# The first modulation projection in two column halves, with the first projection steps between them

## The chip, the cores and the metric

The kernel runs on one core of a Trainium2 chip. The metric is device time in microseconds for one execution. Engines are named as the profile names them: PE (TensorE matmul) and PEld (its weight load), DVE (VectorE), ACT (ScalarE), POOL (GpSimd), SP (the sync engine, which here issues most DMAs).

## What is computed

One encoder layer on two groups of 1024 tokens with 1024 features each. What matters here is its start: a modulation vector from the condition `c`, and the modulated, normalised input that the input projection multiplies.

```python
mod = (jax.nn.silu(c) @ w_ada + b_ada).reshape(B, N_MOD, D_MODEL)[:, :, None, :]
shift1, scale1, gate1, shift2, scale2, gate2 = [mod[:, i] for i in range(N_MOD)]
h = rmsnorm(x, g_pre_mix) * (1 + scale1) + shift1
x = x + gate1 * rmsnorm(token_mixer(h, w_in, ...), g_post_mix)   # token_mixer starts with h @ w_in
h = rmsnorm(x, g_pre_ffn) * (1 + scale2) + shift2
x = x + gate2 * rmsnorm(expert_choice_moe(h, ...), g_post_ffn)
```

`w_ada` is 1024 by 6144 in float32. The first 2048 of its columns give shift1 (0 to 1023) and scale1 (1024 to 2047) and are needed before any `h` exists. The other 4096 are needed later.

## The kernel before

All five engines run hand-written programs in one block, each in its own order, and they meet in counted semaphores. There is no scheduler: the order in the code is the order on each engine. Work is cut along the 1024 features into KC = 8 steps k of 128, and along tokens into quarters q of 512 (q 0 and 1 are the first group).

**SP** issues, in order and from one queue: `c_in`, the first token quarter x(0) (2 MB), the eight pieces `a_w[:, k, :]` of the first modulation weights (L646, 1 MB each, k-th 128 rows, all 2048 columns), and w(0), the first half unit of the input projection weights (L488, 1 MB). Next comes x(1), in the same buffer as x(0): its issue (L482) waits until PE has turned all eight k of x(0) (`turned` 8). Then w(1), the gate weights, the gate biases.

**PE** first does `ada(0, k)` for k 0 to 7 (L1749): four matmuls with M = 2 rows each (the two groups), 512 columns wide, one in each 32-column group of the array, summed over k in bank PO. A pair of k shares one semaphore (`a_first`). Between them, for k 2 to 5, come the transposes of x(0), two k at a time (`turn_x`, L1738; four transposes for each k, into banks 0 and 1 in turn). After them come 8 filler transposes (`keep_awake`), the 16 small transposes that turn the modulation row into columns (L1923), 18 fillers, and then `stream`: for each k the six matmuls of blocks 0 and 1 (L1805), each k waiting for `h_ready`. Before block b of 2 and up, PE waits for `w_lo_ready` of its half unit and for `evac_done` b - 1, since the two banks are used in turn (L1815, L1816). Block 2 is the first to use w(1).

**ACT** squares x(0) in eight pieces (L1036), takes the turned x out of the banks (`take_x`, L1038), takes two of the four row pieces (`a_row_first`), rounds w(0) to `w_hi` (L1018, two pieces), and makes h in place (`make_h`, L1047). The squares of x(1) stand between the h of k 4 to 7 and behind them. Only after that comes its `fill` stream, whose first work is the evacuation of blocks 0 and 1 (L1030).

**DVE** normalises x(0), takes the other two row pieces, adds the bias and makes `scale` (L1571, L1575), then `w_lo` and, for each k, `h_hi` and `h_lo` (L1379, L1381). Then `mean_of(1)`, the `w_lo` of w(1), and the normalising of x(1). **POOL** makes the reciprocal roots (L792) and `w_hi` of w(1) (L803).

Of the kernel before, what the change touches and what calls it, by code (L numbers as in the profile page):

```python
# [8 lines left out]
ALU = mybir.AluOpType  # L9
# [213 lines left out]
def front(nc, io):  # L223

    with ExitStack() as ctx:
# [160 lines left out]
        a_row_ready, a_row_stored = sem("a_row_ready"), several("a_row_stored", 2)  # L386
# [24 lines left out]
        o_loaded, o_hi_ready, o_lo_ready = several("o_loaded", KC), sem("o_hi_ready"), sem("o_lo_ready")  # L411
# [6 lines left out]
        x1_half, h2_half = sem("x1_half"), sem("h2_half")  # L418
# [7 lines left out]
        PX = 7  # L426
        A_ROUNDS = 3
# [48 lines left out]
        def _(sp):  # L476
# [85 lines left out]
            def load_o(c):  # L562
                sp.wait_ge(blk_done, NBLK - 2 * (1 - c))
                for a in range(4):
                    sp.dma_start(o_raw[:, 2 * a:2 * a + 2, c * HALF:(c + 1) * HALF], w_out_view[a, c]).then_inc(o_loaded[4 * c + a], 16)
# [78 lines left out]
            load_x(0)  # L644
            for k in range(KC):
# [368 lines left out]
        def _(act):  # L1014
# [23 lines left out]
            def take_x(k):  # L1038
                act.wait_ge(turned, k + 1)
                nc.scalar.activation(h_raw[:, k, 0:HALF], ps[:, k % 2, :], ACT.Copy).then_inc(xT_ready, 1)  # L1040

            def a_row_first():
                act.wait_ge(a_done, KC)
                for j in range(2):
                    nc.scalar.activation(a_row[32 * j:32 * j + 2, 0, :], ps[32 * j:32 * j + 2, PO, :], ACT.Copy).then_inc(a_row_ready, 1)

            def make_h(q, k):  # L1047
                g, half = q // 2, q % 2
                cut = slice(half * HALF, (half + 1) * HALF)
# [83 lines left out]
            def stream():  # L1133
# [26 lines left out]
                for t in range(N_TILES + OUT_TAIL):  # L1160
# [25 lines left out]
                    if 1 <= t <= N_TILES:  # L1186
                        if t == N_TILES:
                            act.wait_ge(x1_half, 1)
# [25 lines left out]
            for k in range(KC):  # L1214
                take_x(k)
            act.drain()
            a_row_first()
            split_w(0, 0)
            for k in range(KC):
                make_h(0, k)  # L1220
                if k == 1:
                    split_w(0, 1)
                if k >= 4:
                    squares(1, k - 4)
# [133 lines left out]
        def _(dve):  # L1358
# [124 lines left out]
            def stream():  # L1483
# [23 lines left out]
                for t in range(N_TILES + OUT_TAIL):  # L1507
# [9 lines left out]
                    if 1 <= t <= N_TILES:  # L1517
# [4 lines left out]
                        for cut in HALVES_OF_D if t == N_TILES else (slice(0, D),):  # L1522
# [3 lines left out]
                            nc.vector.tensor_tensor(ox[:, j, cut], ox[:, j, cut], h2[:, j, cut], ALU.add).then_inc(x1_ready if cut.stop == D else x1_half, 1)  # L1526
# [22 lines left out]
                    if 1 <= t <= N_TILES:  # L1549
                        dve.wait_ge(or_ready, 2 * t)  # L1550
                        for cut in HALVES_OF_D if t == N_TILES else (slice(0, D),):
                            nc.vector.scalar_tensor_tensor(h2[:, j, cut], ox[:, j, cut], o_r[:, 1:2], rows[g][:, 1, cut], ALU.mult, ALU.mult)
                            dve.drain()
                            nc.vector.tensor_tensor(h2[:, j, cut], h2[:, j, cut], rows[g][:, 2, cut], ALU.add).then_inc(h2_ready if cut.stop == D else h2_half, 1)
# [11 lines left out]
            a_row_first()  # L1566
            dve.wait_ge(cols_loaded, 48)
            dve.wait_ge(mod_turned, 2)
            for g in range(GROUPS):
                turned_mods = ps[:, PS:PS + 4, 0:4 * GROUPS].rearrange("p j (k g) -> p j k g", g=GROUPS)[:, :, :, g]  # L1570
                nc.vector.tensor_tensor(mods[:, :, :, g].rearrange("p w (j k) -> p (w j) k", j=2), turned_mods,  # L1571
                                        b_cols[:, :].rearrange("p (j k) -> p j k", k=4), ALU.add)
            dve.drain()
            for g in range(GROUPS):
# [1203 lines left out]
```

## Time and profile before

| what | value |
|---|---|
| median of 3 runs | 2403.22 us (2403.15 to 2404.04) |
| the profiled execution, its own time | 2404.34 us |
| span in its trace | 2402.6 us |
| PE busy | 2296.1 us (96%) |
| DVE, ACT, POOL busy | 1208.7, 1103.8, 603.2 us |
| mean DMA rate | 213 GB/s |

Before its first matmul PE waits 14.5 us, the longest wait but one that it has. The stretch that the change touches is the first 51 us of the span, 2% of it: until PE begins block 2 at 51.05 us. Everything else (the other blocks, the recurrent and attention parts, the experts) comes later.

### The profile page before, as it was taken

What the parts mean: (1) busy time and instruction counts of PE and PEld (TensorE: products, weight loads), DVE (VectorE), ACT (ScalarE), POOL (GpSimd) and SP (SyncE); (2) the same over time, 40 slices, a digit from 0 to 9 for tenths busy, and PEclk for the clock granted to TensorE, in tenths of its full rate; (3) what the DMA queues carried; (4) which work ended last, traced back from release to release, by engine and by line L of the source; (5) the groups of instructions that cost most, each with busy time, mean ns of one, the idle gap of its engine ahead of it and who ended that gap; (6) DMA issues with size and microseconds to landing.
All of it is one profiled execution on the core that took longest, in us unless ns stands there. A gap on an engine that the chain in (4) does not pass through costs nothing. (4 is left out here: it accounts for less than half of the span.)

```text
span 2402.6 us, 35196 instructions
## 1 busy us (share of the span) xinstructions
PE 2296.1 (96%) x13583; PEld 1915.1 (80%) x13583; DVE 1208.7 (50%) x1881; ACT 1103.8 (46%) x1828; POOL 603.2 (25%) x676
## 2 busy tenths in 40 slices
PE   6999999999999999999947999999999999999997
PEld 4679989777899897667736888888888888888886
DVE  3222334554413346665566555544445556666655
ACT  4223444655433436665543444444444455555552
POOL 3004342443133324430021011111110122222434
PEclk9999999999999999999978999999999999999999
DMA  8835445658454459764547566666666678888785
GB/s 319 259 107 182 145 160 185 191 150 185 122 194 141 162 177 249 228 180 158 170 189 263 204 211 221 214 226 210 207 203 231 216 268 309 322 308 291 284 302 175
DMA packets 239040, 511.49 MB, mean 213 GB/s; under 512 B 36981, under 2 KB 128005, under 8 KB 235825
## 3 DMA queue, kind: packets, MB, share of 16 engines
q1 hardware_dynamic: 190960, 394.78, 49.0%
q0 software_dynamic: 47936, 114.77, 16.0%
q8 instruction: 93, 1.52, 0.3%
q14 instruction: 51, 0.41, 0.1%
HBM read 415.32 MB, written 93.69 MB: 212 GB/s over the span
## 5 line engine op out<-in xcount | busy, mean ns | idle before, releaser
L2492 DVE TENSOR_TENSOR moe_w_lo<-moe_wf,moe_w_hi 128x2048 fp32r<-128x2048 f32 x192 | 439.5, 2292 | 456.6 <-ACT moe_w_hi L2367 450.0
L2367 ACT ACTIVATE moe_w_hi<-moe_wf 128x2048 fp32r<-128x2048 f32 x192 | 367.8, 1916 | 551.4 <-PE moe_acc L2630 550.5
L2630 PE MATMUL moe_acc<-moe_w_hi,moe_x_hi 128*128 128x512 f32 x1024 | 401.7, 392 | 0.9 <-DVE moe_x_lo L2498 0.6
L2630 PE MATMUL moe_acc<-moe_w_hi,moe_x_lo 128*128 128x512 f32 x1024 | 398.9, 390 | 0.0
L2630 PE MATMUL moe_acc<-moe_w_lo,moe_x_hi 128*128 128x512 f32 x1024 | 398.4, 389 | 0.0
L2630 PEld LDWEIGHTS moe_acc<-moe_w_hi,moe_x_hi 128*128 128x128 f32 x1024 | 192.3, 188 | 40.7 <-DVE moe_x_lo L2498 0.8
L2630 PEld LDWEIGHTS moe_acc<-moe_w_hi,moe_x_lo 128*128 128x128 f32 x1024 | 192.2, 188 | 40.3
L2630 PEld LDWEIGHTS moe_acc<-moe_w_lo,moe_x_hi 128*128 128x128 f32 x1024 | 192.4, 188 | 38.9
L1793 PE MATMUL banks<-fr_w_hi,fr_h_hi 128*128 128x256 f32 x768 | 223.2, 291 | 0.0
L1793 PE MATMUL banks<-fr_w_lo,fr_h_hi 128*128 128x256 f32 x768 | 217.0, 283 | 0.0
L1793 PE MATMUL banks<-fr_w_hi,fr_h_lo 128*128 128x256 f32 x768 | 216.9, 282 | 0.0
L1784 PE MATMUL banks<-fr_h_hi,fr_w_hi 128*128 128x512 f32 x496 | 204.3, 412 | 1.9 <-DVE fr_h_lo L1381 1.1
L2630 PE MATMUL moe_acc<-moe_w_hi,moe_h_hi 128*128 128x512 f32 x512 | 199.3, 389 | 0.0
L2630 PE MATMUL moe_acc<-moe_w_hi,moe_h_lo 128*128 128x512 f32 x512 | 199.2, 389 | 0.0
L2630 PE MATMUL moe_acc<-moe_w_lo,moe_h_hi 128*128 128x512 f32 x512 | 199.2, 389 | 0.0
L1784 PE MATMUL banks<-fr_h_hi,fr_w_lo 128*128 128x512 f32 x496 | 194.2, 392 | 0.0
L1784 PE MATMUL banks<-fr_h_lo,fr_w_hi 128*128 128x512 f32 x496 | 193.7, 390 | 0.0
L1030 ACT ACTIVATE fr_stage<-banks 128x512 f32<-128x512 f32 (+1 forms) x114 | 67.3, 590 | 271.9 <-PE banks L1784 146.2
L1362 DVE TENSOR_TENSOR fr_w_lo<-fr_w_raw,fr_w_hi 128x1024 fp32r<-128x1024 f32 x56 | 73.6, 1316 | 208.3 <-ACT fr_w_hi L1018 208.3
L906 POOL DMA_DIRECT2D fr_v<-scratch_vov x224 | 156.5, 740 | 81.9 <-PE banks L1963 80.6
L1793 PEld LDWEIGHTS banks<-fr_w_hi,fr_h_hi 128*128 128x128 f32 x768 | 146.8, 191 | 4.9 <-issue 4.8
L1793 PEld LDWEIGHTS banks<-fr_w_lo,fr_h_hi 128*128 128x128 f32 x768 | 147.0, 191 | 0.1
(294 smaller groups left out, 4083.4 us busy)
## 6 DMA issues: line engine op xcount, KB each, us to landing
moe_wf<-in_w_expert_gate SPq DMA_DIRECT2D x64, 1024.0 KB, 4.9
moe_wf<-in_w_expert_up SPq DMA_DIRECT2D x64, 1024.0 KB, 4.9
moe_wf<-in_w_expert_down SPq DMA_DIRECT2D x64, 1024.0 KB, 5.8
fr_w_raw<-in_w_units SPq DMA_DIRECT2D x28, 1024.0 KB, 7.2
fr_bias<-in_na_bias SPq DMA_DIRECT2D x16, 1520.0 KB, 11.1
fr_a_w<-in_w_ada POOLq DMA_DIRECT2D x16, 1024.0 KB, 9.0
scratch_qk_t<-fr_stage SPq DMA_DIRECT2D x64, 256.0 KB, 2.5
scratch_vov<-fr_stage SPq DMA_DIRECT2D x96, 128.0 KB, 2.2
```

Source lines behind the costliest of these rows:

```text
L906: pool.dma_start(v[j][p0:CHUNK, CH_AT[rb] + n, :], v_view[2, m, r0:r0 + k, cols_, :]).then_inc(nv_loaded[j], 16)
L1030: nc.scalar.activation(out, product, ACT.Copy).then_inc(evac_done, 1)
L1362: nc.vector.tensor_tensor(w_lo[:, h % 2, k, :], w_raw[:, h % 2, k, :], w_hi[:, h % 2, k, :].bitcast(F32), ALU.subtract).then_inc(w_lo_read ...
L1784: mm = nc.tensor.matmul(ps[:, b % 2, :], w[x1][:, slot, k, a * P:(a + 1) * P], h[x2][:, k, t * HALF:(t + 1) * HALF], start=start, stop=stop)
L1793: mm = nc.tensor.matmul(ps[:, b % 2, part * QW:(part + 1) * QW], h[x1][:, k, tile:tile + P], w[x2][:, slot, k, :], start=(k == 0 and i == ...
L2367: nc.scalar.activation(w_hi[:, q, :, :], wf[:, q, :, :], ACT.Copy).then_inc(w_hi_ready, 1)
L2492: nc.vector.tensor_tensor(w_lo[:, q, :, :], wf[:, q, :, :], w_hi[:, q, :, :].bitcast(F32), ALU.subtract).then_inc(w_lo_ready, 1)
L2630: mm = nc.tensor.matmul(acc[:, j, b, :], x[:, g, k, :], w[:, q, a, h * HALF:(h + 1) * HALF], start=(k == 0 and i == 0), stop=(k == KC - 1 ...
```

## The change

The first modulation weights come in two halves. A half is 512 columns of shift1 and the same 512 of scale1, so half 0 gives the modulation of k 0 to 3 and half 1 that of k 4 to 7. SP issues eight half pieces (0.5 MB, in runs of 2 KB instead of 8 KB), then w(0), then the other eight, then x(1) as before behind `turned` 8. Each half is multiplied in four groups of 256 columns (`ada_first`), into bank PO (half 0) and PA = 3 (half 1). The row pieces, the turning and the DVE arithmetic are done once for each half (`a_row_first(half)`, `turn_mods(half)`, `modulation(half)`).

On PE, all of half 0 comes first, then the turning of x(0) for k 0 to 5, then 10 fillers, and then four rounds of: one step of `stream` (k 0 to 3), in rounds 1 and 2 one `turn_x` (k 6, 7), and two k of half 1. On ACT the h of a half follows its `take_x` and one piece of `split_w`, and all squares of x(1) come behind the last h. On DVE `mean_of(1)` moves behind the `w_lo` of w(1). Some semaphores are shared (the half pieces with the later output weights, `row_half` for two uses at the end of the front part), with counts changed to match.

```diff
-            for k in range(KC):
-                sp.dma_start(a_w[:, k, :], ada_view[k, :, 0:4 * HALF]).then_inc(a_first[k // 2], 16)
+                sp.dma_start(ada_part(a_w[:, k, :], 0), ada_part(ada_view[k, :, 0:4 * HALF], 0)).then_inc(a_first[k // 2], 16)
             load_w(0)
+            for k in range(KC):
+                sp.dma_start(ada_part(a_w[:, k, :], 1), ada_part(ada_view[k, :, 0:4 * HALF], 1)).then_inc(a_o_loaded[k], 16)
             load_x(1)
...
+            def ada_first(k, half):
+                if half:
+                    pe.wait_ge(a_o_loaded[k], 16)
+                else:
+                    pe.wait_ge(a_first[k // 2], 32)
+                for j in range(4):
+                    c0 = (j // 2 * 2 + half) * HALF + j % 2 * QW
+                    mm = nc.tensor.matmul(ps[32 * j:32 * j + 2, (PO, PA)[half], 0:QW], c_silu[:, k, :], a_w[:, k, c0:c0 + QW],
+                                          start=(k == 0), stop=(k == KC - 1))
+                mm.then_inc((a_early, a_done)[half], 1)
...
+            for k in range(6):
+                turn_x(0, k)
+                if k == 1:
+                    turn_mods(0)
+            keep_awake(PC[0], 10)
+            for k in range(4):
+                fill.tick(1)
+                if k in (1, 2):
+                    turn_x(0, 5 + k)
+                ada_first(2 * k, 1)
+                ada_first(2 * k + 1, 1)
+            keep_awake(PC[0], 8)
+            turn_mods(1)
+            keep_awake(PA, 18)
```

**ACT, from the first h to the evacuation of block 0, before.** L1054 makes h, L1036 squares x(1), L1030 evacuates a block.

```order
L1054 ACTIVATE fr_h_raw<-fr_h_raw,fr_mods,fr_scale 128x512 [waits fr_scale_ready] x2
L1018 ACTIVATE fr_w_hi<-fr_w_raw 128x1024 [waits fr_w_loaded0]
L1054 ACTIVATE fr_h_raw<-fr_h_raw,fr_mods,fr_scale 128x512 [waits fr_scale_ready] x3
L1036 ACTIVATE banks,fr_ss<-fr_x 128x512 [waits fr_x_loaded]
L1036 ACTIVATE banks,fr_ss<-fr_x 128x512
L1054 ACTIVATE fr_h_raw<-fr_h_raw,fr_mods,fr_scale 128x512 [waits fr_scale_ready]
L1036 ACTIVATE banks,fr_ss<-fr_x 128x512 [waits fr_x_loaded]
L1036 ACTIVATE banks,fr_ss<-fr_x 128x512
```

The same place now (L1065 makes h, L1049 takes turned x, L1055 the row pieces, L1045 squares, L1039 evacuates).

```order
L1065 ACTIVATE fr_h_raw<-fr_h_raw,fr_mods,fr_scale 128x512 [waits fr_scale_ready] x4
L1049 ACTIVATE fr_h_raw<-banks 128x512 [waits fr_turned] x4
L1027 ACTIVATE fr_w_hi<-fr_w_raw 128x1024 [waits fr_w_loaded0]
L1055 ACTIVATE fr_a_row<-banks 2x256 [waits fr_a_done]
L1055 ACTIVATE fr_a_row<-banks 2x256
L1065 ACTIVATE fr_h_raw<-fr_h_raw,fr_mods,fr_scale 128x512 [waits fr_scale_ready] x4
L1045 ACTIVATE banks,fr_ss<-fr_x 128x512 [waits fr_x_loaded]
```

Behind that row stand the other seven squares and then `L1039`, the evacuation of block 0, in both kernels. The squares of x(1) moved from between the h of k 4 to 7 to behind them.

**PE, from the fillers on, now.** L1756 is a filler, L1841 a stream step's matmul (six for each k), L1786 the modulation, L1766 a transpose of x(0).

```order
L1756 MATMUL banks<-fr_ident 128x128 x10
L1841 MATMUL banks<-fr_h_hi,fr_w_hi 128x512 [waits fr_h_ready,fr_w_lo_ready]
...
L1786 MATMUL banks<-fr_a_w,fr_c_silu 2x256 [waits fr_a_o_loaded0]
L1786 MATMUL banks<-fr_a_w,fr_c_silu 2x256 x3
L1786 MATMUL banks<-fr_a_w,fr_c_silu 2x256 [waits fr_a_o_loaded1]
L1786 MATMUL banks<-fr_a_w,fr_c_silu 2x256 x3
L1841 MATMUL banks<-fr_h_hi,fr_w_hi 128x512 [waits fr_h_ready]
...
L1766 MATMUL banks<-fr_ident,fr_x 128x128 [waits fr_xT_ready]
```

Before, all transposes of x(0) stood ahead of the last two k of the modulation, and every stream step behind it:

```order
L1736 MATMUL banks<-fr_ident 128x128 x10
L1758 MATMUL banks<-fr_a_w,fr_c_silu 2x512 [waits fr_a_first3]
L1758 MATMUL banks<-fr_a_w,fr_c_silu 2x512 x3
L1758 MATMUL banks<-fr_a_w,fr_c_silu 2x512 [waits fr_a_first3]
L1758 MATMUL banks<-fr_a_w,fr_c_silu 2x512 x3
L1736 MATMUL banks<-fr_ident 128x128 x8
L1923 MATMUL banks<-fr_ident,fr_a_row 128x2 [waits fr_a_row_ready]
```

The last two transposes of x(0), on which SP's issue of x(1) waits, moved behind stream steps 1 and 2.

## Rows read from the trace of the kernel before

**Rows 1.** The page: PE's busy time, and the chain that ended last.
```profile
PE 2296.1 (96%) x13583; PEld 1915.1 (80%) x13583; DVE 1208.7 (50%) x1881; ACT 1103.8 (46%) x1828; POOL 603.2 (25%) x676
PE 42%; DVE 3%; DMA 2%; issue 1%; POOL 0%; ACT 0%; DVEq 0%; POOLq 0%; ACTq 0%; SPq 0%
```

**Rows 2.** Timeline, PE, 14 to 57 us (start, us, engine line, tiles, idle before).
```profile
14.50 3.59 PE L1758 MATMUL banks<-fr_a_w,fr_c_silu 128*2 128x512 f32 x16 [14.50 <-DMA fr_a_w<-in_w_ada]
...
19.38 1.89 PE L1758 MATMUL banks<-fr_a_w,fr_c_silu 128*2 128x512 f32 x8 [1.07 <-DMA fr_a_w<-in_w_ada]
21.19 1.97 PE L1746 MATMUL banks<-fr_ident,fr_x 128*128 128x128 f32 x8
...
28.23 1.09 PE L1746 MATMUL banks<-fr_ident,fr_x 128*128 128x128 f32 x8
...
30.47 1.90 PE L1758 MATMUL banks<-fr_a_w,fr_c_silu 128*2 128x512 f32 x16
...
37.49 0.47 PE L1805 MATMUL banks<-fr_h_hi,fr_w_hi 128*128 128x512 f32 x1 [1.02 <-DVE fr_h_lo L1381]
...
45.11 0.39 PE L1805 MATMUL banks<-fr_h_hi,fr_w_lo 128*128 128x512 f32 x1
...
49.87 0.39 PE L1805 MATMUL banks<-fr_h_hi,fr_w_lo 128*128 128x512 f32 x1
51.05 0.50 PE L1784 MATMUL banks<-fr_h_hi,fr_w_hi 128*128 128x512 f32 x1 [0.79 <-DVE fr_w_lo L1362]
...
56.63 0.60 PE L1746 MATMUL banks<-fr_ident,fr_x 128*128 128x128 f32 x4
```

**Rows 3.** Windows: us, PE, PEld, DVE, ACT, POOL busy, PEclk, DMA share, GB/s.
```profile
9.00:14.00 5.00, 0.00 (x0) 0.00 (x0) 0.00 (x0) 4.21 (x12) 0.00 (x0) 1.00 1.02 428
14.00:19.00 5.00, 3.81 (x17) 0.61 (x17) 1.99 (x5) 1.57 (x6) 2.74 (x4) 1.00 1.02 426
36.00:40.00 4.00, 2.98 (x16) 2.37 (x15) 3.78 (x8) 3.92 (x6) 0.00 (x0) 1.00 1.03 343
```

**Rows 4.** The two issues of x (L482): first and last start; time to landing.
```profile
L482 SPq DMA_DIRECT2D fr_x<-in_x x2: 389/406/423, 1.2 to 29.3; - x2
...
DMA to landing us min/median/max: 8.1/8.7/9.3
```

**Rows 5.** The same for the two issues of w (L488).
```profile
L488 SPq DMA_DIRECT2D fr_w_raw<-in_w_units x2: 562/1126/1689, 6.1 to 29.8; - x2
...
DMA to landing us min/median/max: 11.6/11.6/11.6
```

**Rows 6.** Timeline, PE: matmuls of 256 columns in four groups, from 73.86 us.
```profile
73.86 0.61 PE L1779 MATMUL banks<-fr_h_hi,fr_wg 128*16 128x256 f32 x8
74.29 0.61 PE L1779 MATMUL banks<-fr_h_lo,fr_wg 128*16 128x256 f32 x8
```

**Rows 7.** Timeline, ACT and DVE, 24 to 37 us.
```profile
24.93 1.08 ACT L1040 ACTIVATE fr_h_raw<-banks 128x512 f32<-128x512 f32 x2 [1.14 <-PE banks L1746]
...
32.43 1.20 ACT L1045 ACTIVATE fr_a_row<-banks 2x512 f32<-2x512 f32 x2 [2.43 <-PE banks L1758]
...
35.02 1.22 DVE L1362 TENSOR_TENSOR fr_w_lo<-fr_w_raw,fr_w_hi 128x1024 fp32r<-128x1024 f32 x1
35.15 1.52 ACT L1054 ACTIVATE fr_h_raw<-fr_h_raw,fr_mods,fr_scale 128x512 f32<-128x512 f32 x2 [0.43 <-DVE fr_scale L1575]
36.16 0.42 DVE L1379 CAST fr_h_hi<-fr_h_raw 128x512 fp32r<-128x512 f32 x1
36.57 1.04 ACT L1018 ACTIVATE fr_w_hi<-fr_w_raw 128x1024 fp32r<-128x1024 f32 x1
36.66 0.69 DVE L1381 TENSOR_TENSOR fr_h_lo<-fr_h_raw,fr_h_hi 128x512 fp32r<-128x512 f32 x1
```

**Rows 8.** Timeline, ACT: first and last piece of the squares of x(0).
```profile
9.39 0.60 ACT L1036 ACTIVATE banks<-fr_x 128x512 f32<-128x512 f32 x1 [6.67 <-DMA fr_x<-in_x]
...
15.54 0.19 ACT L1036 ACTIVATION_READ_ACCUMULATOR banks<-fr_x 128x1 f32 x1
```

**Rows 9.** Timeline, all engines: what stands before block 2 and behind it.
```profile
41.45 2.43 POOL L803 CAST fr_w_hi<-fr_w_raw 128x1024 fp32r<-128x1024 f32 x2 [16.33 <-DMA fr_w_raw<-in_w_units]
...
48.64 2.35 DVE L1362 TENSOR_TENSOR fr_w_lo<-fr_w_raw,fr_w_hi 128x1024 fp32r<-128x1024 f32 x2
48.82 1.93 POOL L792 TENSOR_TENSOR fr_rms<-fr_mean,fr_mhalf 128x4 f32<-128x4 f32 x1 [4.42 <-DVE fr_mean L1369]
49.68 1.21 ACT L1030 ACTIVATE fr_stage<-banks 128x512 f32<-128x512 f32 x2 [1.39 <-PE banks L1805]
...
50.92 2.73 DVE L1373 TENSOR_SCALAR fr_x<-fr_x,fr_rms 128x1024 f32<-128x1024 f32 x4
```

More of the change, by code:

```diff
@@ L1213, in _ @@
                 squares(0, j)
-            for k in range(KC):
[L1215 to L1224, printed above, removed]
+            a_row_first(0)
+            for half in range(2):
+                for k in range(4 * half, 4 * half + 4):
+                    take_x(k)
+                act.drain()
+                split_w(0, half)
+                if half:
+                    a_row_first(1)
+                for k in range(4 * half, 4 * half + 4):
+                    make_h(0, k)
+            for j in range(4):
+                squares(1, j)
             act.wait_ge(cols_loaded, 48)
@@ L1565, in _ @@
             nc.vector.tensor_copy(b_cols[:, :], ps[:, PS, 0:2 * KC])
-            a_row_first()
             dve.wait_ge(cols_loaded, 48)
[L1568 to L1574, printed above, removed]
-                a = nc.vector.scalar_tensor_tensor(scale[:, g, :], mods[:, 1, :, g], 1.0, g_pre[:, :], ALU.add, ALU.mult)
-            a.then_inc(scale_ready, 1)
-            split_w(0, 0)
-            for k in range(KC):
-                split_h(0, k)
-                if k == 1:
+            for half in range(2):
+                a_row_first(half)
+                modulation(half)
+                if half == 0:
+                    split_w(0, 0)
+                for k in range(4 * half, 4 * half + 4):
+                    split_h(0, k)
+                if half == 0:
                     split_w(0, 1)
-            mean_of(1)
             for piece in range(2):
                 split_w(1, piece)
+            mean_of(1)
             for j in range(4):
@@ L1760, in ada, with turn_mods @@
                 mm.then_inc(a_done, 1)
+            def ada_first(k, half):
+                if half:
+                    pe.wait_ge(a_o_loaded[k], 16)
+                else:
+                    pe.wait_ge(a_first[k // 2], 32)
+                for j in range(4):
+                    c0 = (j // 2 * 2 + half) * HALF + j % 2 * QW
+                    mm = nc.tensor.matmul(ps[32 * j:32 * j + 2, (PO, PA)[half], 0:QW], c_silu[:, k, :], a_w[:, k, c0:c0 + QW],
+                                          start=(k == 0), stop=(k == KC - 1))
+                mm.then_inc((a_early, a_done)[half], 1)
+            def turn_mods(half):
+                pe.wait_ge(a_row_ready, 2 * half + 2)
+                for which in range(2):
+                    for k in range(4):
+                        at_ = slice(64 * which, 64 * which + 2)
+                        mm = nc.tensor.transpose(ps[:, MOD_BANKS[half][which], k * GROUPS:(k + 1) * GROUPS], a_row[at_, half, k * P:(k + 1) * P], ident[at_, at_])
+                mm.then_inc(mod_turned, 1)
             def turn_rows(g):
@@ L1867, in turn_h2 @@
                 if t == N_TILES - 1 and not half:
-                    pe.wait_ge(h2_half, 1)
+                    pe.wait_ge(row_half, 2)
                 else:
```

77 lines of the change are left out of this document (40 added, 37 removed).

## The prediction, made before the changed kernel was run

> **What bounds the kernel now.** I read the page first: PE is busy for 96% of the span, and the chain that ended last is almost all matmul where it names an engine [rows 1]. So the time is PE's work plus the few places where PE stands still, and a change at the start is worth exactly what it moves the moment from which PE runs on without a break. Next I read PE's timeline from the start [rows 2]. PE's first matmul comes at 14.50, the last two k of the modulation at 30.47, the first stream step at 37.49, the last matmul of the last step at 49.87, and block 2 begins at 51.05. From there on PE's order is the same in both kernels. So the question is one number: **when does block 2 begin**, against 51.05. The stretch is 51 of 2402.6 us, and 0.2% (4.8 us) is about what a measurement can tell from no change.
>
> The windows show what holds the start: the DMA engines are full, 426 to 428 GB/s from 9 to 19 us [rows 3]. The pairs of modulation weights (2 MB each) end 14.50 and 19.38, so 4.9 us for 2 MB.
>
> **The first stream step, now.** The bytes ahead of it shrink from x(0) plus 8 MB to x(0) plus 4 MB plus w(0).
> - x(0) is there at 9.39 [rows 8]. Four pairs of half pieces, 1 MB each, follow. At the rate of the 8 KB runs a pair takes 2.45 us (4.9 / 2). The new runs are of 2 KB, which no row shows alone. The other bound is the stretch from 36 to 40 us, in which w(1) comes in runs of 1 KB: 343 GB/s, 3.06 us for a pair [rows 3]. I take 2.6, nearer to the first, as x(0) with its 4 KB runs came at about that rate too. Last pair: 9.4 + 10.4 = 19.8 (19.2 to 21.6).
> - Two k of the modulation remain. Four groups of 256 columns take 0.43 us where PE is at speed (start to start) [rows 6]. At the start the same matmuls take double: 3.59 us for two k of 512 columns against 1.90 us later [rows 2]. PE will be idle about a third of the time until then, so I take the slow price, 0.9 each. End of half 0: about 21.5 (20.1 by the early bounds).
> - The transposes of x(0) come only now. Two k take 1.97 us in the slow state, 1.09 later [rows 2]: 23.4. ACT takes k 0 to 3 at 0.54 each [rows 7]; the third and fourth transpose wait for its first two, so the fourth is taken at about 25.5. Then ACT rounds the first piece of w(0), 1.05, which has landed (19.8 + 3.1 = 22.9, as one more MB at 343 GB/s): 26.6. DVE's `w_lo` 1.22, then `h_hi` and `h_lo`, 1.2 from the start of one to the end of the other [rows 7]: 29.0. If PE reaches its speed early, 27.6.
> - So the first stream step starts at S = 28.8, with ends 27.4 and 31.0 (the slow DMA bound). Before: 37.49. That part of the change is worth **8.7 us** if nothing came behind.
>
> **From there to block 2.** What lies behind S is PE's own row of work:
> - A stream step is six matmuls at 0.227 (45.11 to 49.87, 21 of them) [rows 2]: 1.36. Four steps 5.44. Eight k of half 1 at 0.43: 3.44, and two transposes of x(0) at 0.49: 0.98. End of half 1 at S + 9.9 = 38.7. The weights for it landed by about 34, so no wait for data. DVE delivers an h in 1.11, under 1.36.
> - Before, the end of the modulation (32.4) was followed by ACT's next h at 35.15, 2.8 us later [rows 7], with copies of 512 columns and 16 small transposes. With copies and transposes halved I take 2.1: S + 12.0. Four h at 0.75: S + 15.0. DVE adds 1.2 behind the first: PE's step for k 4 at S + 14.0, its last step ends at S + 19.5 = 48.3. Before it was 50.1. **On PE alone the gain has shrunk to 1.8 us**, or 2.8 with the 0.79 us wait at block 2, since PE now does the modulation and two transposes between the steps instead of ahead of them.
> - Block 2 also wants bank 0 evacuated, and that is **ACT's** work, behind all eight squares of x(1), which moved behind the last h. The eight squares take 6.34 us (9.39 to 15.73) [rows 8]. ACT starts them at S + 15.0, ends at S + 21.4, and the evacuation of one block, half of 1.21 [rows 9], ends at S + 22.0. Block 2 starts at **S + 22.1 = 50.9**. Before, ACT had idled 1.39 us ahead of that evacuation [rows 9], so it cost nothing there.
> - Could the squares start at all at S + 15.0? x(1) is issued when the eighth transpose is done, now behind stream step 2: S + 6.8 = 35.6, against 29.35 before. It lands 8.1 to 9.3 us later [rows 4]: S + 14.9 to S + 16.1. I take the first, since the queue has run empty by then, as it was for the first x. The other end costs 1.1 us more.
> - w(1) is issued behind it, at S + 7.2. Before it took 11.6 us behind a backlog [rows 5]. From x(1) on, 3 MB at 428 and 343 GB/s are 8 us and some 2 of start and end: S + 17.2. POOL rounds it, 2.43, DVE's second piece 1.2 behind [rows 9]: S + 21.0 = 49.8. Late too (before it had waited from 43.9 to 48.64 for DVE), but just behind ACT. `mean_of(1)` moving behind these two pieces costs nothing, as the squares end later still.
> - Behind block 2: mean, root (1.93 or less) and normalising (2.73) of x(1) [rows 9] end at S + 26.5 at the latest. PE wants x(1) 5.6 us after the start of block 2 [rows 2], S + 27.7. Covered, with 1.2 us to spare.
>
> The sum: block 2 at 50.9 against 51.05, **0.1 us earlier**. The span becomes 2402.5, the profiled time 2404.2. That execution lies 1.1 us above the median of the runs, so I forecast 2403.1 for the median. The shared semaphores, `row_half` among them, are waited for at the same places with counts that the same instructions reach: nothing. After block 2 all is the same order, shifted as one.
>
> The Trainium skill, page "DMA: Bandwidth & Descriptors", section "Bandwidth", speaks against cutting the loads: it wants 1 MiB or more in a DMA for 75% of peak, and gives 2.0 us plus bytes / 436e3 for one. By that a half piece is an estimated 3.2 us and a whole one 4.4. The rows don't bear it out for queued loads: 2 MB in 4.9 us is 2.45 for a whole piece.
>
> **The rivals.**
> 1. *The start comes early and part of the gain stays.* PE is at speed before the transposes and the half pieces keep the rate of the whole ones: S = 27.4, ACT's tail as above, block 2 at 49.5, 1.5 us earlier: 2401.7. If moreover x(1) were so quick that ACT never waits it stays at that, since ACT is bound by its own row; PE's own end (S + 19.5) can't be reached. For it: ACT's row is short of waits. Against: at the start PE is fed in pieces.
> 2. *Slower: the 2 KB runs come at the rate of the 1 KB ones.* The place is the last pair of half 0. At 3.06 us for a pair, and w(0) and x(1) landing at their late ends, S = 30.7, squares from S + 16.1, block 2 at 53.9: 2.9 us later, 2406.1. It decides against the change from about 2.65 us for a pair on (0.2 us above my 50.9 is all the room). For it: only rows at 1 KB and 4 KB or more exist.
> 3. *Each half piece pays a price of its own.* If every DMA cost a fixed 2 us that the queue doesn't hide, a half piece would take 3.2 us (2.0 and 1.2 of data) and half 0 would end at 35: S = 44, block 2 at 66, about 2418. Against it: the 2.45 us of a whole piece in the rows leaves no room for 2 us. This is what the page "DMA: Bandwidth & Descriptors" of the Trainium skill would give, section "Bandwidth".
> 4. *PE stays slow through the new gaps.* PE waits about 2 us between its fillers and S. If the stream steps and half 1 then run at the doubled price, S to S + 9.9 becomes S + 19.7, and all behind it 10 us later: 2413.
>
> **How the numbers follow.** My forecast, within about 1 us: 0.47. Rival 1: 0.22. Rival 2 (1 to 4.5 us slower): 0.22. Rivals 3 and 4: 0.02 and 0.05. Something larger in the gaining direction that I don't see: 0.02. The likeliest is 2403.1. The range takes in rivals 1 and 2 with the runs' own spread of 0.9 us: 2400.9 to 2406.2. That leaves out 3, 4 and the tails, under 0.2. Faster by over 0.2% (below 2398.4) needs more than the whole gain on PE: 0.03. Slower by over 0.2% (above 2408.0): rivals 3, 4 and the tail of 2, 0.09. Within: 0.88.
>
> **What would show it.** In the profile after: PE's first stream step at 27.4 to 31; half 1 done about 10 us later; the issue of x(1) near 35.6 and a hole in the DMA rate ahead of it; ACT's squares in one row from about 44 to 50; block 2 with a wait of 2 to 3 us that ends with ACT's evacuation, not with `w_lo`. If block 2 waits for nothing, my reading of ACT is wrong. If S is above 31, the runs of 2 KB are. If the two traces differ after block 2 by more than at it, the shift doesn't carry, and the whole argument from one number falls.

## The result, and the profile of the changed kernel

| | before | after |
|---|---|---|
| median of 20 runs | 2403.18 us (2401.22 to 2405.77) | 2407.59 us (2405.29 to 2412.69) |
| the profiled execution, its own time | 2404.34 us | 2407.66 us |
| span in its trace | 2402.6 us | 2405.9 us |
| block 2 begins | 51.05 us | 54.65 us |

The ratio is 1.002 with an interval of 1.0014 to 1.0027: slower by 4.4 us. The forecast was 2403.1 and its range ended at 2406.2, so it was wrong. Block 2 had been forecast at 50.9.

PE's timeline of the changed kernel answers to [rows 2]. Columns: start, us, engine line, tiles, idle before and what ended it.

```profile
14.84 1.89 PE L1786 MATMUL banks<-fr_a_w,fr_c_silu 128*2 128x256 f32 x16 [0.52 <-DMA fr_a_w<-in_w_ada]
17.55 1.89 PE L1786 MATMUL banks<-fr_a_w,fr_c_silu 128*2 128x256 f32 x16 [0.82 <-DMA fr_a_w<-in_w_ada]
20.27 1.89 PE L1786 MATMUL banks<-fr_a_w,fr_c_silu 128*2 128x256 f32 x16 [0.83 <-DMA fr_a_w<-in_w_ada]
...
24.52 2.46 PE L1766 MATMUL banks<-fr_ident,fr_x 128*128 128x128 f32 x12
...
30.77 0.47 PE L1841 MATMUL banks<-fr_h_hi,fr_w_hi 128*128 128x512 f32 x1 [1.85 <-DVE fr_h_lo L1393]
...
32.32 1.04 PE L1786 MATMUL banks<-fr_a_w,fr_c_silu 128*2 128x256 f32 x16
33.30 0.50 PE L1841 MATMUL banks<-fr_h_hi,fr_w_hi 128*128 128x512 f32 x1
...
41.85 1.09 PE L1756 MATMUL banks<-fr_ident 128*128 128x128 f32 x8
...
46.16 0.47 PE L1841 MATMUL banks<-fr_h_hi,fr_w_hi 128*128 128x512 f32 x1 [0.71 <-DVE fr_h_lo L1393]
...
54.65 0.50 PE L1820 MATMUL banks<-fr_h_hi,fr_w_hi 128*128 128x512 f32 x1 [2.79 <-DVE fr_w_lo L1374]
...
60.26 0.60 PE L1766 MATMUL banks<-fr_ident,fr_x 128*128 128x128 f32 x4
```

A reader should take five things from it. The pairs of half pieces come 2.7 us apart. The first stream step starts at 30.77 (S, as in the prediction), 6.7 us before the old 37.49. The four rounds behind it end at 41.85, at S + 11.1. The step for k 4 starts at 46.16, and the last step ends at 51.9. Then PE waits 2.79 us for `w_lo` of w(1), and block 2 begins 3.6 us later than before. From block 2 to the first transpose of x(1) it is 5.6 us, as in [rows 2].

The timeline of the other engines tells who was late. First SP's two issues, which came at 29.35 and 29.78 before:

```profile
38.42 0.37 SPq L488 DMA_DIRECT2D fr_x<-in_x  x1
38.83 0.55 SPq L494 DMA_DIRECT2D fr_w_raw<-in_w_units  x1
```

And what stands ahead of block 2 on POOL, DVE and ACT, the answer to [rows 9]:

```profile
50.36 2.02 POOL L812 CAST fr_w_hi<-fr_w_raw 128x1024 fp32r<-128x1024 f32 x2 [25.21 <-DMA fr_w_raw<-in_w_units]
...
51.43 3.16 DVE L1374 TENSOR_TENSOR fr_w_lo<-fr_w_raw,fr_w_hi 128x1024 fp32r<-128x1024 f32 x2 [2.11 <-POOL fr_w_hi L812]
```
```profile
46.99 0.60 ACT L1045 ACTIVATE banks<-fr_x 128x512 f32<-128x512 f32 x1
...
53.16 0.19 ACT L1045 ACTIVATION_READ_ACCUMULATOR banks<-fr_x 128x1 f32 x1
53.37 1.08 ACT L1039 ACTIVATE fr_stage<-banks 128x512 f32<-128x512 f32 x2
```

w(1) lands at 50.36, 11.5 us after its issue; its `w_lo` is ready at 54.59. ACT's row of squares runs from 46.99 to 53.35 without a gap, and the evacuation of block 0 is done at 53.9. So two chains end within 0.7 us of each other, and the one through w(1) is the later. The windows (columns as in [rows 3]) show the hole that the late issue leaves in the loads:

```profile
14.00:19.00 5.00, 3.65 (x37) 0.97 (x33) 1.93 (x5) 1.63 (x6) 2.68 (x4) 1.00 1.05 387
...
36.00:40.00 4.00, 4.00 (x37) 2.49 (x30) 0.00 (x0) 1.52 (x3) 0.00 (x0) 1.00 0.17 28
```

28 GB/s from 36 to 40 us, against 343 before [rows 3]; and 387 GB/s where the half pieces come (14 to 19 us), against 426 there before [rows 3].

### The profile page after: what moved, and what is told of

Its sections match the earlier page's. It is cut to its first block and busy times, and to the rows that moved or that the text cites. A ratio compares the mean times of both kernels' runs of the same rounds, so it can differ in the third digit from the quotient of the medians.

```text
span 2405.9 us, 35342 instructions
## 1 busy us (share of the span) xinstructions
PE 2301.4 (96%) x13647; PEld 1920.9 (80%) x13647; DVE 1205.0 (50%) x1887; ACT 1104.0 (46%) x1830; POOL 598.3 (25%) x676
## 5 line engine op out<-in xcount | busy, mean ns | idle before, releaser
L1039 ACT ACTIVATE fr_stage<-banks 128x512 f32<-128x512 f32 (+1 forms) x114 | 67.1, 590 | 271.4 <-PE banks L1820 147.0
```

Of the source, the lines that this page charges most:

```text
L1039: nc.scalar.activation(out, product, ACT.Copy).then_inc(evac_done, 1)
```

## The experiments

Beside each ran the kernel before, with medians of 2402.9, 2403.3 and 2402.7 us in the three sets of runs. "Block 2", "turn" and "span" are read from one profiled execution of each, in us; "turn" is the first transpose of x(1), which PE does when block 2 is through. The ratio is the 95% interval against the kernel before beside it.

| variant | from | block 2 | turn | span | median (lowest to highest) | ratio |
|---|---|---|---|---|---|---|
| before | | 51.05 | 56.63 | 2402.6 | 2403.18 | |
| after | | 54.65 | 60.26 | 2405.9 | 2407.59 | 1.0014 to 1.0027 |
| cut_loads | before | 52.96 | 58.54 | 2404.5 | 2404.97 (2402.94 to 2407.73) | 0.9995 to 1.0015 |
| squares_behind | before | 50.82 | 56.39 | 2401.9 | 2403.07 (2399.90 to 2406.35) | 0.9986 to 1.0005 |
| late_x1 | before | 53.13 | 61.05 | 2403.9 | 2406.34 (2404.05 to 2410.45) | 1.0005 to 1.0023 |
| w1_first | after | 54.38 | 61.44 | 2406.5 | 2407.93 (2405.02 to 2410.68) | 1.0006 to 1.0026 |
| turn_early | after | 52.89 | 58.46 | 2404.6 | 2404.59 (2403.49 to 2406.38) | 0.9996 to 1.0015 |
| warm_start | after | 55.45 | 62.58 | 2407.6 | 2409.38 (2406.69 to 2410.55) | 1.0011 to 1.0030 |
| fill_gap | after | 54.83 | 62.00 | 2407.9 | 2406.95 (2403.78 to 2410.69) | 1.0006 to 1.0024 |
| again | after | 54.60 | 61.76 | 2407.3 | 2408.53 (2404.14 to 2410.18) | 1.0011 to 1.0029 |
| hold_clock | after | 55.29 | 60.88 | 2403.9 | 2405.22 (2403.99 to 2406.49) | 1.0002 to 1.0020 |
| best1 | after | 51.44 | 58.59 | 2400.6 | 2403.34 (2400.67 to 2405.88) | 0.9989 to 1.0007 |
| best3 | after | 53.17 | 58.73 | 2403.9 | 2403.23 (2401.61 to 2406.17) | 0.9995 to 1.0013 |
| best5 | after | 50.26 | 56.60 | 2402.2 | 2402.33 (2400.97 to 2406.75) | 0.9993 to 1.0011 |

### What one part costs in the kernel before

**cut_loads** cuts only the loads: each 1 MB piece comes as two half pieces, and all of PE's work stays.

```diff
-                sp.dma_start(a_w[:, k, :], ada_view[k, :, 0:4 * HALF]).then_inc(a_first[k // 2], 16)
+                for half in range(2):
+                    sp.dma_start(ada_part(a_w[:, k, :], half), ada_part(ada_view[k, :, 0:4 * HALF], half)).then_inc(a_first[k // 2], 16)
```

> The kernel before with each of the eight 1 MB pieces issued as two half pieces in runs of 2 KB, both halves of a k one after the other, nothing else changed. Theory (the short runs are slower, 2.7 against 2.45 us for 1 MB): the last pair lands at 32.4 instead of 30.5, the first stream step at 39.4 and block 2 at 53.0. Rival (the runs cost nothing): 30.5, 37.5 and 51.05.

```profile
32.37 1.90 PE L1760 MATMUL banks<-fr_a_w,fr_c_silu 128*2 128x512 f32 x16 [0.73 <-DMA fr_a_w<-in_w_ada]
...
52.96 0.50 PE L1786 MATMUL banks<-fr_h_hi,fr_w_hi 128*128 128x512 f32 x1 [0.77 <-DVE fr_w_lo L1364]
```

The last pair is multiplied from 32.37 instead of 30.47 [rows 2], and block 2 follows 1.9 us later too. So 8 MB in runs of 2 KB cost 1.9 us more than in runs of 8 KB, 0.24 for each MB: half 0 of the changed kernel, 4 MB, pays an estimated 1.0 us. The cause (the runs' length or the number of DMAs, 16 for 8) was not told apart.

**squares_behind** moves only the squares and the mean of x(1), as the change does.

```diff
                 make_h(0, k)
...
-                if k >= 4:
-                    squares(1, k - 4)
+            for j in range(4):
+                squares(1, j)
...
-            mean_of(1)
             for piece in range(2):
                 split_w(1, piece)
+            mean_of(1)
```

> The kernel before with one part of the change alone: ACT's eight squares of x(1) behind the last h instead of between the h of k 4 to 7, and DVE's mean behind the rounding of w(1). Theory (ACT's row costs only because x(1) comes late in the changed kernel): x(1) is here by 38.7, the h are no longer held up, the last h is made by about 43, the squares end at 49.4, the rounding on DVE at about 49, block 2 at 50.2 instead of 51.05, 0.8 earlier. Rival (the move of the squares is itself the loss): block 2 at 52 or later.

```profile
50.82 0.47 PE L1784 MATMUL banks<-fr_h_hi,fr_w_hi 128*128 128x512 f32 x1 [0.17 <-ACT fr_stage L1030]
```

Block 2 begins at 50.82. With x(1) there in time, this move costs nothing. Where S is 37.9, ACT's row just fits. The theory had given it 0.8 us: the profile has 0.2 (0.6 counted from S, which came 0.4 us later here), the medians show no difference.

**late_x1** adds to it one wait on SP, which puts the issue of x(1) and w(1) about where the change put it.

```diff
             load_w(0)
+            sp.wait_ge(h_ready, 1)
             load_x(1)
```

> The kernel of squares_behind with SP's issue of x(1) and w(1) held until the first h is ready, about 37.5 instead of 29.35 us, as late as the change makes it. Theory (the late issue is what the change pays): w(1) lands 11.5 us after its issue at 49.4, POOL and DVE are done at 53.6, ACT's row at about 52.3, block 2 at 53.7, 3.5 later than with squares_behind alone. Rival (the price lies in PE's own order, in the modulation between the stream steps): block 2 stays within 1 us of squares_behind.

The rows are SP's, DVE's and PE's.

```profile
37.44 0.38 SPq L482 DMA_DIRECT2D fr_x<-in_x  x1
...
49.92 3.16 DVE L1363 TENSOR_TENSOR fr_w_lo<-fr_w_raw,fr_w_hi 128x1024 fp32r<-128x1024 f32 x2 [3.64 <-POOL fr_w_hi L804]
```
```profile
53.13 0.79 PE L1785 MATMUL banks<-fr_h_hi,fr_w_hi 128*128 128x512 f32 x1 [3.86 <-DVE fr_w_lo L1363]
```

This is the changed kernel's ending without its beginning: issue at 37.44, w(1) at POOL at 48.85, `w_lo` ready at 53.0, a wait of 3.86 us. Block 2 comes 2.3 us later than in squares_behind (3.5 had been expected), and x(1)'s first transpose 4.7 us later; the extra is the clock, below. The time rises by 3.3 us between the two medians.

### Which chain holds block 2 in the changed kernel

**w1_first** turns the two issues round.

```diff
-            load_x(1)
             load_w(1)
+            load_x(1)
```

> The changed kernel with w(1) issued ahead of x(1), so that it no longer waits for the transposes of x(0). Theory: block 2 (54.65 us in the changed kernel) is held by two chains that end close together, w(1) through POOL and DVE (54.6) and ACT's squares of x(1) and its evacuation of block 0 (53.95). With w(1) early the second is left: block 2 at 54.1, 0.6 us earlier. Rival: the late weights are the whole loss; then block 2 starts when PE is done with block 0 and 1, at 51.7.

```profile
49.52 2.36 DVE L1374 TENSOR_TENSOR fr_w_lo<-fr_w_raw,fr_w_hi 128x1024 fp32r<-128x1024 f32 x2
```
```profile
54.38 0.76 PE L1820 MATMUL banks<-fr_h_hi,fr_w_hi 128*128 128x512 f32 x1 [2.25 <-ACT fr_stage L1039]
```

`w_lo` is ready at 51.9, 2.7 us earlier, and block 2 gains only 0.3: it now waits for ACT's evacuation. The theory's 54.1 was met, the rival's 51.7 was not. Freeing one of two nearly equal chains gives almost nothing. (The granted clock fell behind S here, as told below, so that half 1 ended 0.3 us later than in after; the right neighbour is again, where it fell too, and against it the gain is 0.2.)

**turn_early** puts all eight transposes of x(0) ahead of the first stream step, in banks of their own, so that SP issues x(1) early. The transposes of k 6 and 7 then no longer wait for ACT, and PE has 6 fillers there instead of 10.

```diff
-        first_bank = lambda k: k % 2 if k < 4 else 6 + k % 2
+        first_bank = lambda k: (0, 1, 0, 1, 6, 7, 5, 2)[k]
...
-            for k in range(6):
+            for k in range(KC):
                 turn_x(0, k)
...
             for k in range(4):
                 fill.tick(1)
-                if k in (1, 2):
-                    turn_x(0, 5 + k)
```

> The changed kernel with the last two transposes of x(0) moved ahead of the first stream step (into banks 5 and 2), so that x(1) and w(1) are issued at about 29 instead of 38.4 us. Theory (late issue plus ACT's row): the first stream step stays at 30.8, half 1 ends at about 40.9 instead of 41.9, ACT's squares still follow the last h and end at 52.3, block 2 at 53.0, 1.6 us earlier. Rival (the late issue is the whole loss): block 2 when PE is done, 50.5.

The rows are POOL's and DVE's, then PE's.

```profile
43.45 2.22 POOL L812 CAST fr_w_hi<-fr_w_raw 128x1024 fp32r<-128x1024 f32 x2 [18.30 <-DMA fr_w_raw<-in_w_units]
```
```profile
43.60 1.16 DVE L1391 CAST fr_h_hi<-fr_h_raw 128x512 fp32r<-128x512 f32 x1 [0.88 <-ACT fr_h_raw L1065]
44.84 1.37 DVE L1393 TENSOR_TENSOR fr_h_lo<-fr_h_raw,fr_h_hi 128x512 fp32r<-128x512 f32 x1
```
```profile
46.35 0.47 PE L1841 MATMUL banks<-fr_h_hi,fr_w_hi 128*128 128x512 f32 x1 [2.12 <-DVE fr_h_lo L1393]
...
52.89 0.47 PE L1820 MATMUL banks<-fr_h_hi,fr_w_hi 128*128 128x512 f32 x1 [0.85 <-ACT fr_stage L1039]
```

x(1) is issued at 28.36, the hole is gone (408 GB/s or more from 34 to 38 us) and both chains are earlier: block 2 at 52.89, 1.8 us before the changed kernel's. The median is 1.7 us above that of the kernel before beside it, where the change had been 4.4 above (the two intervals just overlap). All that came from this one move. But w(1) now lands at 43.45, exactly when DVE makes the h of k 4, and POOL's cast slows it: 1.16 and 1.37 us for operations of 0.42 and 0.69 [rows 7]. PE's step for k 4 thus starts at 46.35, no earlier than in the changed kernel.

### Is it PE's slow start?

**warm_start** puts 70 fillers ahead of the modulation, so that PE should be at speed when half 0 comes.

```diff
             pe.wait_ge(c_ready, 1)
+            keep_awake(PC[0], 70)
             for k in range(KC):
                 ada_first(k, 0)
```

> The changed kernel with 70 filler transposes on PE ahead of its first modulation matmul. Theory: the slow matmuls and transposes from 12 to 27 us are on the path of the first stream step; with PE at speed the first half ends about 0.9 us earlier and the transposes another 0.8, first stream step at 29.1 instead of 30.8, block 2 at 52.9. Rival: ACT and the loads set the first stream step, which stays at 30.5 or later, and block 2 at 54.4.

```profile
17.66 1.04 PE L1786 MATMUL banks<-fr_a_w,fr_c_silu 128*2 128x256 f32 x16 [1.68 <-DMA fr_a_w<-in_w_ada]
21.27 1.50 PE L1786 MATMUL banks<-fr_a_w,fr_c_silu 128*2 128x256 f32 x16 [2.57 <-DMA fr_a_w<-in_w_ada]
...
30.56 0.47 PE L1841 MATMUL banks<-fr_h_hi,fr_w_hi 128*128 128x512 f32 x1 [1.85 <-DVE fr_h_lo L1393]
```

The third pair takes 1.04 us, so PE was at speed; but then it is done early, waits 2.57 us, and the last pair takes 1.50, with a granted clock of 0.93, 0.50 and 0.71 in the windows of 2 us from 20 to 26. That pair also landed 1.0 us later than in after, for a reason that I did not find. S is 30.56 and block 2 stands at 55.45, so the theory's numbers were not met. But the test is not clean, because of that late landing: from the start of the last pair to S it is 9.3 us here and 10.5 in after. That PE's slow start cost after part of its S is shown better by the executions compared further below.

**fill_gap** has 25 fillers instead of 10 ahead of the first step, to close the 1.85 us before S, behind which the granted clock fell in w1_first and warm_start.

```diff
-            keep_awake(PC[0], 10)
+            keep_awake(PC[0], 25)
```

> The changed kernel with 25 instead of 10 filler transposes ahead of the first stream step, so that PE doesn't stand still before it (1.85 us in the profile). In two of the profiles so far the granted clock fell to 0.50 right behind that gap and PE lost about 1.5 us. Theory: in the changed kernel that happens in part of the executions and is the 1 us by which its median lies further from the kernel before (4.4) than its profiled span does (3.3); with the gap filled no fall in the profile, block 2 at 54.6 as before, and a median 1 us lower, 2406.5, with fewer runs above 2409. Rival: the fall has another cause; median 2407.6 and the same spread.

```profile
28.16 3.08 PE L1756 MATMUL banks<-fr_ident 128*128 128x128 f32 x25
31.00 0.48 PE L1841 MATMUL banks<-fr_h_hi,fr_w_hi 128*128 128x512 f32 x1
...
54.83 0.47 PE L1820 MATMUL banks<-fr_h_hi,fr_w_hi 128*128 128x512 f32 x1 [2.73 <-DVE fr_w_lo L1374]
```

Block 2 stands at 54.83 with a wait of 2.73 as before. The granted clock stays at 1.00 from 28 to 40 us, but falls to 0.50 from 56 to 58, behind that wait, and x(1)'s transpose comes 7.2 us behind block 2 instead of 5.6. The median is not clearly lower than after's. The theory was half right: with this gap filled nothing fell behind it, but block 2 did not move, and the fall behind block 2's own wait stayed.

### The clock behind the new wait

**again** is the changed kernel, unaltered.

> The changed kernel once more, unaltered, beside hold_clock on the same chip. In five of the eight other profiles in which PE waits over 2 us ahead of block 2 the granted clock fell to 0.50 behind that wait and the next 2 to 5 us of PE's work took double; in the changed kernel's own profile it didn't. Theory: it falls in part of its executions, too. Block 2 at 54.6, transposes of x(1) 5.6 us behind it where the clock holds and about 7.1 where it falls; median about 2407.6 with a spread of several us. Rival: the changed kernel never loses the clock there and its median follows the trace alone, 3.3 over the kernel before.

In this expectation "five of the eight other profiles in which PE waits over 2 us" should read: of eight profiles by then, five had such a wait at block 2, and the clock fell in all five.

First PE at block 2 in this execution and ACT's evacuation, then the window behind block 2, then the same window of the execution shown above.

```profile
53.86 1.09 ACT L1039 ACTIVATE fr_stage<-banks 128x512 f32<-128x512 f32 x2
```
```profile
54.60 0.59 PE L1820 MATMUL banks<-fr_h_hi,fr_w_hi 128*128 128x512 f32 x1 [2.26 <-DVE fr_w_lo L1374]
```
```profile
56.00:58.00 2.00, 2.00 (x7) 1.52 (x6) 2.00 (x4) 0.00 (x0) 2.00 (x3) 0.50 0.98 390
```
```profile
56.00:58.00 2.00, 2.00 (x11) 1.63 (x10) 1.94 (x3) 0.00 (x0) 2.00 (x4) 1.00 0.94 357
```

Same program, same block 2 within 0.05 us, but 0.50 (the 1.2 GHz level) and 7 matmuls in one, 1.00 (2.4 GHz) and 11 in the other. Block 2 takes 7.2 us instead of 5.6. The two chains end 0.1 us apart here (block 0 evacuated at 54.4, `w_lo` at 54.5). The clock was also at 0.50 from 32 to 34, where PE worked on behind the 1.84 us gap before S; that gap of 1.84 or 1.85 us is in five profiles, and the clock fell behind it in four (again, w1_first, warm_start, hold_clock), where half 1 then took 12.6 us from S instead of 11.1. Only after's own profile kept the clock both there and at block 2 without fillers at either.

So the program has executions of both kinds. How wide its runs spread (6.0 us here, 7.4 in after) says little by itself, since the kernel before spread over 4.6 to 9.9 us in its four samples. The mean granted clock of each run, which is on record too, says more: the six slowest of after's 20 runs (2409.4 us and more) all have 0.986, the other 14 have 0.987 to 0.989 and a median of 2407.4, and of 97 runs of the kernel before only one is below 0.988 (0.987, its slowest, 2410.9). So the slowest runs of after go with a lower clock. In again this is less clear (its highest, 2410.2, has 0.988), at which place a run lost the clock is not recorded, and without the six the median would hardly move.

**hold_clock** puts 26 fillers into the wait at block 2.

```diff
                 for b in range(2, NBLK):
                     hu = BLOCKS[b][1]
+                    if b == 2:
+                        keep_awake(PA, 26)
```

> The changed kernel with 26 filler transposes on PE between its eighth stream step and block 2, so that PE works through the 2.8 us wait. Theory: block 2 at 54.6 as before, no fall of the granted clock from 54 to 60 us, the first transpose of x(1) 5.6 us behind block 2, and a median about 1 us under that of again, 2406.5, with fewer runs above 2409. Rival (the spread has nothing to do with the clock at this wait): the same median and spread as again.

```profile
52.46 3.00 PE L1756 MATMUL banks<-fr_ident 128*128 128x128 f32 x26
```
```profile
56.00:58.00 2.00, 2.00 (x11) 1.61 (x10) 1.30 (x2) 0.00 (x0) 2.00 (x3) 1.00 0.95 373
```

PE has no idle time there, the clock stays at 1.00, and although block 2 begins 0.7 us later (55.29), x(1)'s transpose comes 0.9 earlier (60.88, 5.6 behind). The runs lie between 2403.99 and 2406.49, 2.5 us wide; seven of again's eleven lie above the highest of them, and none has a mean granted clock below 0.988, where again's go down to 0.986. The gain of 3.3 us between the medians is more than the 1 to 1.5 that the clock at block 2 explains: of the 3.4 us between the two profiles 0.9 are there at x(1)'s transpose and 2.5 come behind it. The intervals of the two ratios overlap, and the rest is open.

The profiles together: of seven with a wait of over 2 us (2.25 to 3.86) at block 2 (after, again, w1_first, warm_start, fill_gap, late_x1, best1) the granted clock fell behind it in six, all but after's own. Of the four with a wait of 0.85 us or less (before, cut_loads, squares_behind, turn_early) it fell in none, nor in the three with fillers there (hold_clock, best3, best5).

### Can the split pay at all?

**best1** joins turn_early and w1_first, makes the first half of `w_hi` earlier on ACT, puts 16 fillers before S, and lets transposes of k 4 and up run without waiting for ACT.

```diff
                     take_x(k)
+                    if k == 1:
+                        split_w(0, 0)
...
-                else:
+                elif k < 4:
                     need(pe, xT_ready, k - 1)
```

> The changed kernel put right where the runs point: w(1) issued ahead of x(1), all transposes of x(0) ahead of the first stream step, the first piece of w(0) rounded between ACT's second and third take, 16 fillers. Theory: first stream step at 28.9, half 1 done at 39.2, last h at 44.2, ACT's squares until 50.7 and the evacuation of block 0 at 51.2, block 2 at 51.4, that is 3.3 earlier than the change and 0.3 later than before: ACT's row alone gives back what PE has won. Rival (the late loads were all): block 2 when PE is done, at about 49.

ACT's row, then PE's.

```profile
44.31 0.60 ACT L1045 ACTIVATE banks<-fr_x 128x512 f32<-128x512 f32 x1
...
50.70 1.09 ACT L1039 ACTIVATE fr_stage<-banks 128x512 f32<-128x512 f32 x2
```
```profile
24.42 2.84 PE L1769 MATMUL banks<-fr_ident,fr_x 128*128 128x128 f32 x24
...
51.44 0.76 PE L1823 MATMUL banks<-fr_h_hi,fr_w_hi 128*128 128x512 f32 x1 [2.25 <-ACT fr_stage L1039]
```

Half 1 ends at 39.18 and block 2 begins at 51.44, as forecast. PE is 2.7 us earlier than in after, and ACT's eight squares and the evacuation behind them are what it waits for: 2.25 us, with the clock at 0.50 from 52 to 54 behind it.

**best3** adds 20 fillers before block 2.

> best1 with 20 fillers at the same place. Block 2 at 51.4 as in best1, where the clock fell behind a wait of 2.25 us and the first transpose of x(1) came 7.15 us later. Theory: 5.6 instead, 1.5 us won in the profile, median 2402.5, level with the kernel before. Rival: as best1, 2403.3.

```profile
24.31 4.87 PE L1769 MATMUL banks<-fr_ident,fr_x 128*128 128x128 f32 x24
```

The same 24 transposes take 4.87 us here and 2.84 in best1: in this execution PE kept its doubled times until 28.4, in the other it left them at 24.1. So half 1 ended 1.7 us later (40.92) and block 2 began at 53.17. The clock held and x(1)'s transpose came 5.6 behind. The median did not move against best1 (2403.23 to 2403.34), so the expected gain was not to be seen.

**best5** goes back to best1 and evacuates blocks 0 and 1 ahead of the last two squares of x(1), with 6 fillers.

```diff
-            for j in range(4):
+            for j in range(3):
                 squares(1, j)
             act.wait_ge(cols_loaded, 48)
+            evac(0)
+            evac(1)
+            squares(1, 3)
```

> best1 with ACT's evacuation of blocks 0 and 1 ahead of the last two squares of x(1), and 6 fillers ahead of block 2. Theory (ACT's row is what holds block 2 in best1): six squares end at 49.1, block 2 at 49.9, 1.5 earlier; x(1) is normalised late, at 56.4, so that PE waits 0.9 us at its first transpose, which comes at 56.5 against 57.0 with best3: half a us won, median 2402.0. Rival: block 2 stays at 51.4, held by something other than ACT.

```profile
49.52 1.08 ACT L1039 ACTIVATE fr_stage<-banks 128x512 f32<-128x512 f32 x2
```
```profile
50.26 0.47 PE L1825 MATMUL banks<-fr_h_hi,fr_w_hi 128*128 128x512 f32 x1
...
56.60 0.66 PE L1771 MATMUL banks<-fr_ident,fr_x 128*128 128x128 f32 x4 [0.62 <-DVE fr_x L1390]
```

Block 2 begins at 50.26, 0.8 earlier than in the kernel before, and then PE waits 0.62 us for the normalised x(1): its transpose comes at 56.60, before at 56.63. The last of the gain went one step further back. 2402.33 against 2402.67 beside it: no difference that can be told.

## Why the prediction was wrong, step by step

**The frame held.** Block 2 was the right number: it moved by 3.6 us and the span by 3.3. The whole start gain is given back before it, as said. What failed is the sizes, all in one direction, and with them the answer to which chain holds block 2. Of the 3.75 us between the forecast 50.9 and the measured 54.65, S is 2.0 and the stretch from S to the end of half 1 is 1.2: together they carry ACT's row from 50.8 to 53.9. The last 0.7 is w(1)'s chain, which was put ahead of ACT's and ended behind it.

- **The first stream step.** Forecast S = 28.8, measured 30.77, in the range of 27.4 to 31.0. The last pair lands at 20.27 (19.8 said): the pair's price was 2.7, not 2.6, and cut_loads shows it alone. I had leaned on x(0), whose runs of 4 KB came "at about that rate too", 426 GB/s. They did not. While x(0) comes, before (columns as in [rows 3]):

```profile
4.00:6.00 2.00, 0.00 (x0) 0.00 (x0) 0.00 (x0) 0.00 (x0) 0.12 (x1) 1.00 1.03 397
6.00:8.00 2.00, 0.00 (x0) 0.00 (x0) 0.00 (x0) 0.00 (x0) 0.00 (x0) 1.00 1.02 393
```

  That is 2.65 us for 1 MB, the price from which on I had written that the change loses. The larger part of the error is PE: its matmuls took double until 26.3, and the sum had no term for the eight small transposes of the modulation that stand between those of x(0) (23.99 to 24.52), so ACT's fourth take ended at 27.1, not 25.5. How long the doubled times last differs by execution: in the four profiles with the same work ahead of S they end at 23.4 (w1_first), 23.9 (again), 24.4 (hold_clock) and 26.3 (after), and S comes at 29.5, 29.7, 30.0 and 30.8, in the same order. So up to 1.2 of the 2.0 us depend on the execution, and the earliest S is still 0.7 behind the forecast. w1_first, where after has the line at 24.52 above:

```profile
24.09 1.09 PE L1766 MATMUL banks<-fr_ident,fr_x 128*128 128x128 f32 x8
```

- **S to the end of half 1.** Forecast 9.9, measured 11.1. Two k of half 1 take 0.98 us, not 0.86, and a stream step with other work on both sides 1.5 to 1.6, not 1.36 (30.77 to 32.32, 33.30 to 34.79). I had taken both prices from rows in which the same matmul follows itself.
- **The issue of x(1) and w(1).** Forecast S + 6.8 and S + 7.2, measured S + 7.7 and S + 8.1, by the same rounds.
- **w(1)'s chain, the step that named the wrong holder.** I gave w(1) 10.0 us to land by adding bytes over rates; it took 11.5 (10.8 to 11.5 in the five profiles of this order), as much as in [rows 5] with a backlog. The windows show more lost at both ends than my 2 us: 111 and 168 GB/s from 39 to 41 us, and 28 from 49 to 50, ahead of the landing at 50.36; between 46 and 49 it was 274 to 360, not always the 343 of the sum. Then POOL's cast and DVE's `w_lo` took 4.2 us, not 3.8, since two pieces cost DVE 3.16 beside POOL's cast and 2.35 alone [rows 9]. Together with S (2.0) and the issue (0.9) the chain is 4.8 us late: 54.6 for 49.8. I had put it 1.0 us ahead of the end of ACT's row, called that "just behind ACT", and made nothing of how near it was. late_x1 shows the chain alone: with the issues 8.6 us later (37.44 for 28.84) and nothing else changed against squares_behind, block 2 waits for `w_lo` and comes 2.3 us later. What the misjudged landing alone cost the changed kernel is less, 0.2 to 0.7 us, since ACT's row ends so near.
- **ACT's row.** Forecast to end at S + 22.0 = 50.8, measured S + 23.1 = 53.9. The row itself was priced rightly (eight squares 6.36 us, 6.34 said); it is late by S and by half 1. It ends 0.7 ahead of the other chain, and w1_first shows that it would hold block 2 at 54.4 in its stead. So "bound by ACT" was wrong for this profile, by 0.7 us, and right once w(1) is earlier.
- **Rivals.** Rival 1 fell: S was never at 27.4 (28.9 at the earliest, in best1). Rival 2 came nearest in size (block 2 at 53.9) and had half its mechanism: the half pieces do cost more, about 1.0 us (estimated from cut_loads), but at 387 GB/s and not at 343. Rival 3 fell: 2.7 us for two queued half pieces. (Its formula stands on the page of the Trainium skill that is named there, but in the section "Anatomy of one DMA — SWDGE (gpsimd) path", for one DMA issued from GpSimd, and SP issues these; the section "Bandwidth" has the rule of 1 MiB.) Rival 4 had the right kind and the wrong place and price. It said that PE stays slow through the gap before S and that this costs 10 us. In again the clock did fall behind S: S came 1.05 us earlier than in after, and half 1 ended 0.5 later (42.35). That is 1.5 us, not 10, and block 2 was the same.
- **What I did not have.** I read a wait at block 2 as costing its own length. Behind a wait of over 2 us there the granted clock fell to 0.50 in six profiles of seven, and then block 2 costs 1.5 us more (2.3 in late_x1). Rows of before could not show it: its wait there is 0.79. How much of the 4.4 us between the medians is the clock stays open. The 4.4 and the 3.3 of the profiles differ mostly because the profiled execution of before lies 1.2 us above its median while that of after, in which the clock held, lies at its own (2407.66 for 2407.59). hold_clock supports that the clock costs something in other executions and does not settle its size.

Open besides: from x(1)'s first transpose to the end of the span before and after take 2346.0 and 2345.6 us, so the shift carries, but the profiles as a whole differ there by up to 4.1 us (2342.0 in best1, 2343.0 in hold_clock, 2346.1 in turn_early). None of this is the clock at block 2, and nothing here explains it. A span from one profile can't settle a difference of that size.

## What to carry to other kernels

Splitting a load so that an engine starts earlier pays only if everything that the engine next waits for also starts earlier. List each chain that ends at the meeting point, and treat those within 1 us of each other as equal: here removing one (w1_first) gained 0.3 us, and moving the issue of the next load, which shortens both (turn_early), gained 1.8.

A load that is issued when an engine is done with a buffer should not have that engine's new work put ahead of its issue. And a new wait of a few us on TensorE may cost more than its length: look at the granted clock behind it, in more than one execution, since the same program shows both.

## What the runs showed that I had not expected

- **Doubled matmul times with a granted clock of 1.00.** At the start two k of half 0 take 1.89 us, and the same 16 matmuls 1.04 later; 24 transposes take 4.87 or 2.84, while the clock column reads 1.00 in after, best1 and best3. So there the column doesn't tell PE's speed; the duration of one matmul does. The end of the doubled times, read from single matmuls, lies between 23.4 us (w1_first) and 28.4 (best3, fill_gap), 5 us apart in executions of like programs, and S follows it.
- **POOL's cast slows DVE beside it.** 0.42 to 1.16 us and 0.69 to 1.37 us for the two halves of an h (turn_early), 2.35 to 3.16 for two pieces of `w_lo` (w1_first and after). The Trainium skill, page "GPSIMD Engine Reference", section "Specifications", says that the two engines share their way into SBUF and that DVE's operations with two inputs there, or in a fast mode, suffer from it; it gives no size. These rows agree, with 1.3 to 2.8 times.
- **Fillers ahead of everything didn't keep PE at speed**: idle for 2.57 us, it took 1.50 instead of 1.04 for the next pair, at a granted clock of 0.93 and then 0.50 (warm_start).
